# A top-k search on float bits with its marks in PSUM, and two more blocks selected in the stage that hosts the search

## What is computed

```
isc = where(admissible, isc, -inf)
top_val, top_idx = top_k(isc, 256)
s = q_lat . c_kv[top_idx] * scale - slope * |t - top_idx|     (softmax over the selected)
```

## Time and profile before

| | us |
|---|---|
| median of 3 runs (lowest, highest) | 3581.16 (3580.63, 3583.1) |
| the profiled execution, time | 3581.63 |
| the profiled execution, span from first to last instruction | 3579.8 |
| mean granted TensorE clock of it | 0.969 |
| TensorE busy / VectorE busy / ScalarE busy / GpSimd busy | 3300.6 / 2098.5 / 1902.5 / 831.9 |
| halves stage, from to | 1914.1 to 2428.3 |
| latents stage, from to | 2428.3 to 2569.4 |

### The profile page before, as it was taken

How to read it: one execution, slowest core, us unless ns; L and a number is a source line. 1 busy time by engine, 2 the same in 40 slices (tenths; PEclk the granted TensorE clock), 3 DMA queues, 4 the chain that set the end, 5 groups by cost and what they waited for, 6 DMA issues and landing times. The chain is left out here.

```text
span 3579.8 us, 90327 instructions
## 1 busy us (share of the span) xinstructions
PE 3300.6 (92%) x36861; PEld 2899.3 (81%) x36861; DVE 2098.5 (59%) x4831; ACT 1902.5 (53%) x3804; POOL 831.9 (23%) x948
## 2 busy tenths in 40 slices
PE   5899999989999999997988999997689999999899
PEld 5777899988788877876766898896678888888787
DVE  7100100008799984331398999996877777777322
ACT  5222211116688873221486766665468888888311
POOL 3222200001298880001103523523410000000000
PEclk9999999999999999998998999998899999999999
DMA  5333321139523314347222436426653333331432
GB/s 200 112 117 117 129 84 62 49 91 227 164 56 85 85 46 162 127 146 230 82 59 74 145 95 200 134 78 200 211 155 86 85 86 97 85 91 49 153 115 87
DMA packets 368043, 416.92 MB, mean 116 GB/s; under 512 B 51744, under 2 KB 272800, under 8 KB 366368
## 3 DMA queue, kind: packets, MB, share of 16 engines
q1 hardware_dynamic: 302880, 318.55, 30.8%
q10 hardware_dynamic: 64768, 92.81, 7.2%
HBM read 247.21 MB, written 164.10 MB: 115 GB/s over the span
## 5 line engine op out<-in xcount | busy, mean ns | idle before, releaser
L1433 PE MATMUL s_o<-s_v,s_pT 128*64 128x65 f32 (+1 forms) x13056 | 440.1, 224 | 9.7 <-issue 6.8
L230 PE MATMUL s_acc<-s_wh,s_hT 128*128 128x256 f32 (+1 forms) x1408 | 428.3, 304 | 8.5 <-ACT s_parts L658 4.5
L1433 PEld LDWEIGHTS s_o<-s_v,s_pT 128*64 128x64 f32 x13056 | 404.6, 138 | 28.3 <-issue 8.1
L232 PE MATMUL s_acc<-s_wh,s_hT 128*128 128x256 f32 (+1 forms) x1408 | 427.3, 303 | 0.0
L231 PE MATMUL s_acc<-s_wl,s_hT 128*128 128x256 f32 (+1 forms) x1408 | 427.2, 303 | 0.0
L230 PE MATMUL s_acc<-s_hT,s_wh 128*128 128x512 f32 x880 | 349.5, 397 | 54.8 <-DVE s_wl L334 26.2
L1596 ACT ACTIVATE s_probs<-s_probs,s_nmx 128x512 f32<-128x512 f32 (+3 forms) x640 | 388.7, 662 | 12.0 <-DVE s_nmx L1661 12.0
L1645 DVE CUSTOM_DVE_ANT_0 s_probs<-s_s,s_scores 128x512 f32<-128x512 f32 (+3 forms) x640 | 364.3, 607 | 8.9 <-issue 5.1
L2413 DVE TENSOR_SCALAR_CACHE_REDUCE s_scratch<-s_scores,s_thr 128x384 uint8<-128x384 f32 (+4 forms) x320 | 365.3, 1209 | 1.1
L231 PE MATMUL s_acc<-s_hT,s_wh 128*128 128x512 f32 x880 | 347.6, 395 | 0.0
L232 PE MATMUL s_acc<-s_hT,s_wl 128*128 128x512 f32 x880 | 345.4, 392 | 0.0
(11 more groups left out here) (279 smaller groups left out, 7138.4 us busy)
## 6 DMA issues: line engine op xcount, KB each, us to landing
fm<-s_parts ACTq DMA_DIRECT2D x120, 512.0 KB, 2.8
s_y<-y SPq DMA_DIRECT2D x32, 640.0 KB, 5.8
y<-s_g SPq DMA_DIRECT2D x18, 1024.0 KB, 5.8
s_q<-fm SPq DMA_DIRECT2D x32, 512.0 KB, 6.7
kc<-s_parts SPq DMA_DIRECT2D x32, 512.0 KB, 3.3
s_w<-in_o_fm SPq DMA_DIRECT2D x25, 512.0 KB, 4.5
s_w<-in_o_w_in SPq DMA_DIRECT2D x12, 1024.0 KB, 5.3
s_qh<-fm SPq DMA_DIRECT2D x42, 256.0 KB, 3.2
```

Source lines behind the costliest of these rows:

```text
L230: nc.tensor.matmul(out, sh, mh, start=(j == 0), stop=False)
L232: ins = nc.tensor.matmul(out, sl, mh, start=False, stop=(j == n - 1))
L1433: last = nc.tensor.matmul(o_ps[half * HD:(half + 1) * HD, 0:w], pT[half][:, x0:x0 + HD], v[:, g.u.kbs[g.a + x], vc:vc + w], start=(g.first ...
```

## The change

1. The search works on the float's bits themselves. `found` starts as all ones; round i tries `found` exclusive-or a mask (all ones, then bit 30 down to 0) and keeps it where enough scores reach it. `cand` is then a float at once, and `as_float` with its three instructions and the shift of the bit are gone from the round. After the rounds one copy and two new instructions (`as_key`) make the keys that `settle` expects.
2. `found`, `passed` and a copy of `most` lie in the last bank of `spare` (`marks`). The signs of the rounds' passes go to SBUF instead, as bf16.
3. `EARLY` is 8: blocks 6 and 7 are selected in the halves stage. They are wider than the scratch of 1024 columns, so `choose_wide` does them in two pieces, 14 instructions each. `choose_two` for them leaves the latents stage, and the means and norms of tiles 8 to 15 come ahead of the first `choose_two`.
4. `after` is 22 and the last sign passes go four to a slot: the rounds' passes are spread over 157 slots, and the last 14 start at `gone` = 163, that is at e = 51.

```diff
@@ -511,6 +511,7 @@
         rows = [t[:].bitcast(F32) for t in parts]
         acc = [sc.ps(f"acc{k}", [P, BANK]) for k in range(4)]
         spare = sc.ps("spare", [P, 4 * BANK])
+        marks = spare[:, 3 * BANK:4 * BANK].bitcast(U32)
         w_in = sc.sems("w_in", 3)
         set_up = sc.sem("set_up")
         w_hi = sc.sem("w_hi")
@@ -597,7 +598,9 @@
                     if u + 2 < NU:
                         split(u + 2)
-            block.vector(beside)
+            @block.vector
+            def _(dve):
+                beside(dve, marks)
             @block.tensor
             def _(pe):
@@ -925,19 +928,18 @@
                 for t in range(4, 8):
                     low_part(t)
                 search.adjust(dve, search.EARLY, search.NB)
-                for k in range(4):
+                for q in range(4, NP):
+                    mean(q)
+                for q in range(4, NP):
+                    normalize(q)
+                for k in range((search.NB - search.EARLY) // 2):
                     n = search.EARLY + 2 * k
                     def low_parts():
-                        for t in range(4 + 4 * k, 8 + 4 * k):
+                        for t in range(8 + 4 * k, 12 + 4 * k):
                             low_part(t)
-                    search.choose_two(dve, n, even, rank, low_parts if k in (1, 2) else None)
-                    if k == 0:
-                        for q in range(4, NP):
-                            mean(q)
-                        for q in range(4, NP):
-                            normalize(q)
+                    search.choose_two(dve, n, even, rank, low_parts if k in (0, 1) else None)
             @block.gpsimd
             def _(pool):
@@ -2352,17 +2354,19 @@
     NB = NT - B0
     ND = 10
     NA = NB - ND
-    EARLY = 6
-    PER = 7
+    EARLY = 8
+    PER = 4
+    MASKS = [0xFFFFFFFF] + [1 << n for n in range(30, -1, -1)]
     def __init__(self, nc, sc, scores):
         self.nc, self.scores = nc, scores
         self.scratch = sc.sb("scratch", [P, 2, PIECE])
         junk = self.scratch[:, 0, :].bitcast(U8)
+        self.signs = self.scratch[:, 1, :].bitcast(BF16)
         self.junk = [junk[:, k * S:(k + 1) * S] for k in range(2)]
         self.neg_dist = sc.sb("neg_dist", [P, S])
-        self.best, self.bit, self.cand, self.flip, self.thr, self.enough = (
-            sc.sb(name, [P, self.NB], U32) for name in ("best", "bit", "cand", "flip", "thr", "enough"))
+        self.best, self.cand, self.flip, self.thr, self.enough = (
+            sc.sb(name, [P, self.NB], U32) for name in ("best", "cand", "flip", "thr", "enough"))
         self.high, self.low = (sc.sb(name, [P, self.NA], U32) for name in ("high", "low"))
         self.cnt = sc.sb("cnt", [P, self.ND])
         self.balance = sc.sb("balance", [P, self.NB])
@@ -2385,15 +2389,19 @@
     def width(self, n):
         return (n + self.B0 + 1) * P
-    def start(self, dve):
-        v = self.nc.vector
+    def start(self, dve, marks):
+        v, NB = self.nc.vector, self.NB
+        self.found, self.passed = marks[:, 0:NB], marks[:, NB:2 * NB]
+        self.most_p = marks[:, 2 * NB:3 * NB].bitcast(F32)
         for b in range(self.B0, NT):
             v.memset(self.scores(b)[0:HD, b * P + HD:(b + 1) * P], NEVER)
         for n in range(self.NB):
             v.memset(self.most[:, n:n + 1], self.width(n) - 2 * TOPK)
-        v.memset(self.best[:], 0)
-        self.link(dve, v.memset(self.bit[:], SIGN))
+            v.memset(self.most_p[:, n:n + 1], self.width(n) - 2 * TOPK)
+        self.link(dve, v.memset(self.cand[:], 0))
+        self.link(dve, v.tensor_scalar(self.found, self.cand[:], 0xFFFFFFFF, None, ALU.bitwise_xor))
+        self.started = self.links
     def as_float(self, dve, src):
@@ -2402,26 +2410,31 @@
         self.link(dve, v.tensor_scalar(self.flip[:], self.flip[:], SIGN, None, ALU.bitwise_or))
         self.link(dve, v.tensor_tensor(self.thr[:], src[:], self.flip[:], ALU.bitwise_xor))
+    def as_key(self, dve, src):
+        v = self.nc.vector
+        self.link(dve, v.tensor_scalar(self.flip[:], src[:], 31, SIGN, ALU.arith_shift_right, ALU.bitwise_or))
+        self.link(dve, v.tensor_tensor(src[:], src[:], self.flip[:], ALU.bitwise_xor))
     def bits(self, dve, first, last):
         v, ND, NB, NA = self.nc.vector, self.ND, self.NB, self.NA
         for i in range(first, last):
-            self.link(dve, v.tensor_tensor(self.cand[:], self.best[:], self.bit[:], ALU.bitwise_or))
-            self.as_float(dve, self.cand)
+            self.link(dve, v.tensor_scalar(self.cand[:], self.found, self.MASKS[i], None, ALU.bitwise_xor))
             for n in range(ND):
                 if n >= 2:
                     dve.wait_ge(self.counted, i * ND + n - 1)
                 v.tensor_scalar(self.junk[n % 2][:, 0:self.width(n)], self.scores(n + self.B0),
-                                self.thr[:, n:n + 1].bitcast(F32), None, ALU.is_ge, ALU.add,
+                                self.cand[:, n:n + 1].bitcast(F32), None, ALU.is_ge, ALU.add,
                                 accum_out=self.cnt[:, n:n + 1]).then_inc(self.counted, 1)
-            v.tensor_scalar(self.bit[:], self.bit[:], 1, None, ALU.logical_shift_right)
             dve.wait_ge(self.counted, i * ND + ND)
-            v.tensor_scalar(self.enough[:, 0:ND], self.cnt[:], TOPK - 0.5, None, ALU.is_ge).then_inc(self.ch, 1)
+            v.tensor_scalar(self.passed[:, 0:ND], self.cnt[:], TOPK - 0.5, None, ALU.is_ge).then_inc(self.ch, 1)
             dve.wait_ge(self.balanced, i * NA + NA)
-            v.tensor_tensor(self.enough[:, ND:NB], self.balance[:, ND:NB], self.most[:, ND:NB], ALU.is_le
+            v.tensor_tensor(self.passed[:, ND:NB], self.balance[:, ND:NB], self.most_p[:, ND:NB], ALU.is_le
                             ).then_inc(self.ch, 1)
             self.links += 2
             dve.wait_ge(self.ch, self.links)
-            self.link(dve, v.copy_predicated(self.best[:], self.enough[:], self.cand[:]))
+            self.link(dve, v.copy_predicated(self.found, self.passed, self.cand[:]))
+        self.link(dve, v.tensor_copy(self.best[:], self.found))
     def balances(self, act, upto, signs):
@@ -2431,17 +2444,17 @@
         NA, ND = self.NA, self.ND
         for k in range(self.given, upto):
             if k < 32 * NA:
-                n = ND + k % NA
+                n, thr, out = ND + k % NA, self.cand, self.signs
                 if k % NA == 0:
-                    act.wait_ge(self.ch, k // NA * self.PER + 5)
+                    act.wait_ge(self.ch, k // NA * self.PER + self.started + 1)
             else:
-                n = k - 32 * NA
+                n, thr, out = k - 32 * NA, self.thr, signs
                 if n == 0:
                     act.wait_ge(self.ch, self.settled)
             if k >= 1:
                 act.wait_ge(self.balanced, k)
-            self.nc.scalar.activation(signs[:, 0:self.width(n)], self.scores(n + self.B0), ACT.Sign, scale=-1.0,
-                                      bias=self.thr[:, n:n + 1].bitcast(F32),
+            self.nc.scalar.activation(out[:, 0:self.width(n)], self.scores(n + self.B0), ACT.Sign, scale=-1.0,
+                                      bias=thr[:, n:n + 1].bitcast(F32),
                                       accum_out=self.balance[:, n:n + 1]).then_inc(self.balanced, 1)
         self.given = max(self.given, upto)
@@ -2452,6 +2465,7 @@
         v, ND, NB = self.nc.vector, self.ND, self.NB
         best, cand = self.best[:, ND:NB], self.cand[:, ND:NB]
+        self.as_key(dve, self.best)
         v.tensor_copy(self.cand[:, 0:ND], self.best[:, 0:ND])
         v.tensor_scalar(self.high[:], best, 16, None, ALU.logical_shift_right)
         self.link(dve, v.tensor_scalar(self.low[:], best, 0xFFFF, None, ALU.bitwise_and))
@@ -2532,6 +2546,34 @@
     def choose(self, dve, n, even, rank):
         for step in self.steps(n, even, rank):
             self.link(dve, step())
+    def choose_wide(self, dve, n, even, rank):
+        v, L, H = self.nc.vector, self.width(n), PIECE
+        t = self.thr[:, n:n + 1].bitcast(F32)
+        room, room_left = self.room[:, n:n + 1], self.cnt[:, 0:1]
+        def rank_equal(x0, x1):
+            ev, rk = even[:, 0:x1 - x0], rank[:, 0:x1 - x0]
+            self.link(dve, v.tensor_scalar(ev, self.scores(n + self.B0)[:, x0:x1], t, None, ALU.is_equal))
+            self.link(dve, v.tensor_tensor_scan(out=rk, data0=ev, data1=ev, initial=0.0, op0=ALU.add, op1=ALU.max))
+        def keep(x0, x1, left):
+            sc_b, ev, rk = self.scores(n + self.B0)[:, x0:x1], even[:, 0:x1 - x0], rank[:, 0:x1 - x0]
+            self.link(dve, v.tensor_scalar(rk, rk, left, 2.0 ** -126, ALU.is_gt, ALU.mult))
+            self.link(dve, v.scalar_tensor_tensor(out=ev, in0=sc_b, scalar=t, in1=rk, op0=ALU.subtract, op1=ALU.is_lt))
+            self.link(dve, v.scalar_tensor_tensor(out=sc_b, in0=ev, scalar=MASKED,
```

(21 more changed lines are left out.)

## The result

The changed kernel takes 3595.65 us (median of 6 runs, 3592.32 to 3600.92) against 3581.07 for the kernel before beside it (6 runs, 3577.2 to 3584.82). The ratio is 1.0035, with an interval of 1.0022 to 1.0048. It is **slower by 14.6 us**; the forecast was 3578.7, and the range ended at 3587. The profiled execution took 3592.32, with a span of 3590.5.

The account below looks back on a forecast made before the run. The prediction took the sign passes' slots, 2.72 us an event, to become the rounds' bound. Halves stage +3.5 and latents stage -6.2 gave -2.7 us, 3581.6 to 3578.9; with the median 0.5 lower it said 3578.7, range 3572 to 3587.

Parts of the forecast that it names:

- Room there is: Search rounds: VectorE's 12.0 us a round fits inside the slots' 13.35, so the slots become the bound.
- 2.72 us an event: Halves stage: TensorE's time for a row-major event in the kernel before, used as a constant for the changed kernel.
- G = 10.5: Halves stage: TensorE comes 10.5 us forward as stalls from late thresholds go; bounds 0 and 12.
- The marks in PSUM free the small instructions: Search rounds: PSUM operands end VectorE's stalls beside GpSimd, some 32 of 56 us on L2424 and L2416.
- rival A: Search rounds: stalls beside GpSimd stay despite PSUM operands, a round takes 13.7 us, G about 5; 3584 us, chance 0.12.
- the farther memory: Search rounds: marks and signs move to each engine's farther memory; each round loses a little, the sum nothing.
- The tail: Halves stage after event 51: 9.6 + 0.4 us, six blocks 30.4, wide blocks 20.4; VectorE ends at 2442.2 - G.
- the 9 us that I had named as a sign: Halves stage: VectorE idle 9 us before `adjust`, listed among what would show the forecast right.
- Stage +3.5: Halves stage: it ends 3.5 us later than before, VectorE's end at 2431.7 against 2428.2.
- Latents, -6.2: Latents stage: moving two blocks' chooses out and norms ahead gains 6.2 of 16.0 us; bounds 4 and 12.
- Sum -2.7: Both stages together: +3.5 in the halves stage and -6.2 in the latents stage, -2.7 us.
- Rival B: Halves stage: TensorE doesn't come forward, through denser ScalarE passes or a late threshold; +7.8 us, 3589, chance 0.10.

Follow-up runs that it names:

- e11: The kernel after with 64 unused bytes ahead of hT, restoring the operands' distance of the kernel before; ratio 0.9996 to the kernel before, two stages 646.5 us.
- e7: The kernel before with the new search alone, sign passes to SBUF, old slots and addresses; ratio 0.9975 to the kernel before, two stages 636.6 us.
- e1: The kernel after with an unused 14-word tile where `bit` stood, so weights return to their old address; ratio 1.0001 to the kernel before, two stages 649.4 us.
- e10: e1 run once more, unchanged, for a second trace; one execution, 3585.2 us, two stages 649.4 us.
- e16: e1 with found values, marks and limits in small SBUF tiles instead of the PSUM bank; ratio 1.0031 to the kernel before, two stages 660.3 us.
- e9: The kernel after run once more, unchanged, for a second trace; one execution, 3590.1 us, two stages 661.1 us.
- e3: The kernel before with the rounds' sign passes written to SBUF, old search and addresses; ratio 1.0008 to the kernel before, two stages 647.6 us.
- e15: e7 run once more, unchanged; 3578.36 us, ratio 0.9978 to the kernel before, two stages 644.5 us.
- e4: e1 with the rounds' sign passes over slots that end 30 before the last instead of 22; ratio 0.9964 to the kernel before, two stages 638.3 us.
- e14: e4 run once more, unchanged; 3574.24 us, ratio 0.9959 to the kernel before, two stages 639.6 us.
- e2: The kernel before with an unused 14-word tile ahead of `bit`, moving the weights 64 bytes higher; ratio 1.0038 to the kernel before, two stages 662.4 us.

## Why the prediction was wrong

**The step that failed** is "Room there is", with "2.72 us an event": I took TensorE's price of an event over into the changed kernel, and with it G = 10.5. It cost 2.85 in the first half and 2.85 to 2.88 in the second, and event 51 came 2.7 us later after the stage's first split than in the kernel before, not 10.5 sooner (465.5 and 462.8). That put the stage's end 16.9 us later and not 3.5, and the two stages at +8.2 and not -2.7. Nothing in the diff touches TensorE, and I had looked only at what it waits for. The removed tile moved its weights. Against e11, the same change at the old distance, VectorE ended 13.5 us later after the stage's start (526.4 and 512.9): about 11 from row-major units, and some 3 from the 20 column units, which took 11.16 us each in place of 10.99.

The Trainium skill would not lead one to expect this: by TensorE: Matmul & The Clock Gate (Step-by-step: what each phase is for), loading the next weights takes no SBUF read bandwidth from the running matmul, and by SBUF — State Buffer (Who interferes with whom), TensorE waits for nobody. Here the measurement decides: with the same instructions a matmul took 113.3 or 117 to 120 ns by the distance of its two operands. Why stays open: whether it is the two reads that meet was not measured.

**What stood, by the same steps**, where the distance is the old one:

- *Stalls, G = 10.5.* The last of GpSimd's starts for a unit, counted from the stage's first split, came 10.8 us sooner than before in e11, 11.2 in e7. With a slower first half it was 7.5 (e1, row-major units) and 8.7 (e10, column units).
- *The marks in PSUM free the small instructions.* Right, and e16 shows that it is the place. So rival A was wrong; an instruction beside GpSimd's work is the measure that the trace of before lacked. The trace agrees with the Trainium skill's rule on the shared port (SBUF — State Buffer, Who interferes with whom): 376 to 598 ns with all tensors of these instructions in SBUF, 172 to 180 with one in PSUM. Of the loss that the prediction allowed for the farther memory nothing shows: 166 to 180 ns is what such an instruction has in SBUF undisturbed (167 to 175 in the kernel before).
- *The tail.* From the end of event 51 to the first choose 9.6 + 0.4 us were forecast; the kernel after, e1, e9, e10 and e11 all have 9.95 to 9.97 to `adjust`, and 0.2 more. VectorE's idle time ahead of `adjust` is another thing: 9.97 in the kernel after, where TensorE was late, and 2.7 in e11, so the 9 us that I had named as a sign came by luck. Six blocks 30.4: 30.39 (2394.22 to 2424.61). Wide blocks 9.7 and 10.7: 9.73 and 10.67. Stage +3.5: e11 has +3.4 (512.9 against 509.5 before). TensorE's stall of 3.4: 2.9 in e1, in two parts, hidden as said.
- *Latents, -6.2.* About right; the -8.7 of the kernel after and the -8.6 of e11 hold some luck. From where ScalarE is free for the roots to the first `choose_two` for blocks 8 and 9 it is 11.7 to 11.8 us in all five traces with the old order and 5.1 in all thirteen with the new one, 6.7 sooner. From there to the stage's end it is 1.1 longer (80.4 to 80.7 for 79.3 to 79.4). The rest is when ScalarE gets free: 47.9 us after the stage's start in the kernel after and 51.1 in the kernel before, but that moves between executions, from 47.3 (e3) to 53.0 (e15) with the old order and from 47.6 to 50.0 with the new. TensorE's lead doesn't set it: in the kernel after TensorE ends the halves stage 12.9 us ahead of VectorE, and e9 has the same lead and 50.0.
- *Sum -2.7.* Two stages of e1 and e10: -2.3; of e11: -5.2. In time e1 is 1.0001 of the kernel before. "Same" would have been right for this change at the old distance.
- *The parts.* Alone they give -9 and +16 us, together at the old distance 0 and not +7; the intervals nearly allow that. The lengths of the two stages do add: 636.6 + 665.6 - 651.7 = 650.5 (658.4 with e15 for e7), and e1 and e10 have 649.4. The slots that bind were worth 11 us more (e1 to e4, 649.4 to 638.3).

Rival B named the right place and sign, "TensorE doesn't come forward", and had the right mechanism behind it, the last sign passes that hang on event 51. It looked for the cause in ScalarE, for which TensorE waited 1.8 us. It also stopped at 3589, since it took the events' own price as fixed.

The two stages of the kernel after are 8.2 and 9.4 us longer than before's in its two traces, the medians differ by 14.6. The rest lies outside them, within what executions differ by there, and stays unexplained. That a half runs at 21.76 or at 22.61 in different executions (six units, 5 us), as e1, e4, e14 and e15 show, is part of the spread at the old distance.

## What to carry to other kernels

A change that adds or drops a tile moves every tile allocated behind it, in stages it never names. Before a comparison, pin the addresses of the big operands with an unused tile (here 64 bytes were 0.4%), or the address is timed with the idea. Carry no engine's unit price over untested only because the diff doesn't touch that engine. Its busy share hides such a change, 20.00 of 20 us in both kernels; the count of instructions in an equal stretch at an equal clock shows it, 179 against 169.

## What the runs showed that I had not expected

- A row-major matmul of 256 columns costs 113.3 ns at best, and 117.3 to 120.0 with its operands at other distances, at a granted clock of 1.00 and with no wait in the profile. All instructions beside it were the same (e2).
- The same program with the same addresses runs a half of the stage at 21.76 or at 22.61 us a unit, and holds that rate through all row-major units of the half. What sets it is not known.
- VectorE's small comparison L2428 takes 598 ns in SBUF beside GpSimd and 172 with its result in PSUM; its input lies in SBUF both times. As the second small instruction behind the counts it took 167 in SBUF.
- The same program had ScalarE free for the roots of the latents stage 49.0 us after the stage's start in one execution (e7) and 53.0 in another (e15). A term of a few us there can't be read from one pair of traces.
